# Key products of the sample group: eight of 512 columns over all eight pages instead of sixteen of 256 in two halves

## What is computed

```python
pidx = jnp.minimum(idx, past - 1)
phys = page_table[jnp.arange(Bd)[:, None, None], pidx // ps]
ks = jnp.where(in_past, cache_k[l, phys, off], gather_rows(k_new, nidx))
...
logits = jnp.einsum('bqhd,bqkhd->bqhk', q, ks).astype(jnp.float32) * HEAD_DIM ** -0.5
logits = jnp.where(valid[:, :, None, :], logits, NEG_INF)
p = jax.nn.softmax(logits, axis=-1).astype(vs.dtype)
return jnp.einsum('bqhk,bqkhd->bqhd', p, vs)
```

## Time and profile before

| | |
|---|---|
| median of 3 runs | 1124.06 us (1121.25 to 1125.43) |
| profiled execution, own time | 1125.45 us |
| span of the profiled execution | 1123.7 us |
| TensorE busy | 1038.7 us, 92% |
| VectorE busy | 625.8 us, 56% |
| ScalarE busy | 291.6 us, 26% |
| key products, line 1588 | 1024 instructions, 65.6 us busy |
| value products, line 1652 | 1024 instructions, 69.4 us busy |
| page loads | 512 of 256 KB; 4.4 us (keys) and 4.5 us (values) from issue to landing, median |

### The profile page before, as it was taken

How to read it: one execution, slowest core, us unless ns; L and a number is a source line. 1 busy time by engine, 2 the same in 40 slices (tenths; PEclk the granted TensorE clock), 3 DMA queues, 4 the chain that set the end, 5 groups by cost and what they waited for, 6 DMA issues and landing times.

```text
span 1123.7 us, 18202 instructions
## 1 busy us (share of the span) xinstructions
PE 1038.7 (92%) x6082; PEld 536.1 (48%) x6082; DVE 625.8 (56%) x1999; ACT 291.6 (26%) x614; POOL 171.4 (15%) x292
## 2 busy tenths in 40 slices
PE   6999998899989999989999999979999999998994
PEld 3445444344654455555453644434456445554541
DVE  4237995497785244431550779846868825353233
ACT  3221113311322423421422111142114233242131
POOL 9620100011210000001825010000112000000000
PEclk9999999899999989989999999979999998999998
DMA  8534666446866654455643268653688565445511
GB/s 268 161 115 146 198 230 228 135 161 233 303 226 217 210 172 151 145 187 172 196 127 93 97 194 275 195 169 109 219 278 307 179 210 209 150 151 188 183 61 56
DMA packets 106510, 205.24 MB, mean 183 GB/s; under 512 B 15495, under 2 KB 23894, under 8 KB 106418
## 3 DMA queue, kind: packets, MB, share of 16 engines
q1 hardware_dynamic: 87250, 150.25, 39.5%
q0 software_dynamic: 19168, 53.84, 15.3%
HBM read 194.00 MB, written 10.14 MB: 182 GB/s over the span
## 4 chain that ended last, share of the span: by engine, by line
PE 76%; DVE 11%; SPq 4%; ACT 3%; issue 3%; DMA 2%; DVEq 0%; ACTq 0%
PE bank L1485 34%; PE bank L1760 10%; PE bank L1459 6%; PE bank L1588 5%; PE bank L1652 5%; DVE r L1020 3%; SPq L610 3%; PE bank L1788 2%; PE bank L1718 2%; PE bank L1729 2%; DMA pg<-in_cache_k_dram 2%; PE bank L1814 1%; PE bank L1552 1%; PE bank L1700 1%; DVE sh L1114 1%
## 5 line engine op out<-in xcount | busy, mean ns | idle before, releaser
L1485 PE MATMUL bank<-wr,ht 128*128 128x512 f32 (+1 forms) x1024 | 431.3, 576 | 0.3 <-ACT sh L906 0.3
L1485 PEld LDWEIGHTS bank<-wr,ht 128*128 128x128 f32 x1024 | 192.1, 192 | 210.7 <-issue 205.7
L1020 DVE TENSOR_SCALAR_CACHE_REDUCE r<-r,sel_i 128x1088 bf16<-128x1088 f32 (+3 forms) x248 | 187.4, 793 | 3.6
L694 POOL DMA_DIRECT2D wr<-in_w_in_dram x64 | 45.8, 719 | 431.4 <-PE bank L1485 391.6
L610 POOL DMA_DIRECT2D pg<-in_cache_kidx_dram x128 | 68.8, 540 | 49.2 <-issue 44.1
L1459 PE MATMUL bank<-wr,ht 128*64 128x256 f32 (+1 forms) x640 | 74.7, 390 | 1.1 <-DVE ht L1404 1.1
L1652 PE MATMUL bank<-pg,rs 128*32 128x256 f32 x1024 | 69.4, 415 | 0.2 <-DMA pg<-in_cache_v_dram 0.2
L1588 PE MATMUL bank<-pg,r 128*32 128x256 f32 x1024 | 65.6, 396 | 3.9 <-DMA pg<-in_cache_k_dram 2.4
L694 POOL DMA_DIRECT2D wr<-in_w_out_dram x16 | 11.4, 713 | 339.3 <-PE bank L1485 235.8
L1459 PEld LDWEIGHTS bank<-wr,ht 128*64 128x64 f32 x640 | 45.7, 144 | 28.6 <-issue 9.7
L1760 PE MATMUL bank<-wr,gr 128*128 128x512 f32 x128 | 58.1, 596 | 0.0
(11 more groups left out here) (262 smaller groups left out, 1272.6 us busy)
## 6 DMA issues: line engine op xcount, KB each, us to landing
pg<-in_cache_k_dram SPq DMA_DIRECT2D x256, 256.0 KB, 4.4
pg<-in_cache_v_dram SPq DMA_DIRECT2D x256, 256.0 KB, 4.5
wr<-in_w_in_dram POOLq DMA_DIRECT2D x56, 512.0 KB, 4.7
wr<-in_w_out_dram POOLq DMA_DIRECT2D x16, 512.0 KB, 4.6
r<-in_x_prompt_dram SPq DMA_DIRECT2D x8, 512.0 KB, 6.8
pg<-in_cache_kidx_dram POOLq DMA_DIRECT2D x128, 32.0 KB, 2.1
pg<-in_cache_kidx_dram SPq DMA_DIRECT2D x128, 32.0 KB, 2.2
wr<-in_w_in_dram POOLq DMA_DIRECT2D x8, 256.0 KB, 5.4
```

The costliest lines, as they stand in the source:

```text
L694: pool.dma_start(W[n % 2][:, n4 * 2:n4 * 2 + 2, 0:w], src[:, n4 * 2:n4 * 2 + 2, :])\
L1020: ins = nc.vector.tensor_scalar(junk[i][0:m, 0:part.shape[1]], part, sc, None, ALU.is_ge, ALU.add, accum_out=CNT[0:m, i:i + 1])
L1485: mm = pe.matmul(b[0:m, 0:w], HT[:, k, rt * P:rt * P + m], weights[k], start=(k == 0), stop=(k == KC - 1))
```

## The change

The step waits for all four groups at its start, makes eight products of 512 columns, each over all eight page places of the ring for its sequence (four pieces of 128 columns), and adds 4 to `page_group_used` after the last one. The new view `KEYS` names these places. Nothing else moves: the value steps, the loads and the list are the same.

```diff
+        KEYS = pg[:, :].rearrange("p (u t e c n) -> p u t e c n", u=2, t=2, e=2, c=NC4)
...
                 bk = act_bank(l, "s", p, j)
-                for u in range(2):
-                    two = []
+                for g in range(4):
+                    assert group(l, GROUP[s] + g) == 2 * g
+                for k in range(2):
                     for par in range(2):
-                        s0 = group(l, GROUP[s] + 2 * u + par)
-                        two.append(pg[:, s0 * DA:(s0 + 2) * DA].rearrange("p (e c n) -> p e c n", e=2, c=NC4))
-                    for k in range(2):
-                        for par in range(2):
-                            for e in range(2):
-                                r0, q0 = par * NS + e * HW, (2 * p + par) * NS + e * HW
-                                mm = pe.matmul(bk[r0:r0 + HW, u * 256:(u + 1) * 256], QBX[:, 2 * e + k, q0:q0 + HW],
-                                               two[par][:, :, 2 * e + k, :], start=(k == 0), stop=(k == 1),
-                                               tile_position=(0, r0), skip_group_check=True)
-                            if k == 1:
-                                mm.then_inc(group_used, 1)
+                        for e in range(2):
+                            r0, q0 = par * NS + e * HW, (2 * p + par) * NS + e * HW
+                            mm = pe.matmul(bk[r0:r0 + HW, :], QBX[:, 2 * e + k, q0:q0 + HW], KEYS[:, :, par, :, 2 * e + k, :],
+                                           start=(k == 0), stop=(k == 1), tile_position=(0, r0), skip_group_check=True)
+                mm.then_inc(group_used, 4)
```

## The result

The changed kernel takes **1131.03 us** (median of 7 runs, 1129.80 to 1138.13) against 1124.06 us before (7 runs, 1120.74 to 1127.17). The ratio is 1.0078, with a 95% interval of 1.0054 to 1.0103: it is slower, by 0.8%. Forecast were 1135.4 us and slower. The profiled execution took 1131.03 us, its span is 1129.3 us, 5.6 us more than before.

The account below looks back on a forecast made before the run. TensorE was taken as the bound (76% of the chain). Waits 8.4 - products 0.3 + clock 3.2 = +11.3 us on 1125.45 us gave 1136.8 us; with the runs' median 1.4 us lower, 1135.4 us, range 1127 to 1142.

Parts of the forecast that it names:

- The shape of the products: Key steps: 4 rounds of 512 columns instead of 8 of 256 save 0.01 us a step, 0.3 us in all.
- Rival 3: Key products: fixed cost per instruction decides, saving at most 4.6 us; not slower, perhaps faster (1120.3 us); chance 0.06.
- rival 4: Key products: reading four separate 128-column pieces runs slower; at half the rate 55 us more, 1190 us; chance 0.02.
- The late release: After each key step pages are given back 0.87 us later, so all landings after it move by 0.87 us.
- The waits: Key steps wait for late pages at eight places, four in each layer: +8.4 us in sum.
- the eight steps that were named: Key steps at 107.85, 145.11, 172.33, 392.86, 655.93, 693.18, 720.13 and 939.93, each starting or ending 0.21 to 1.74 us later.
- The step at 107.85: Second key step: last page landing at 108.4 before the change, start moved to 109.45, +1.60 us.
- The cover of the value steps: Value steps after key steps: four longer waits, 3.5 us, hidden by later waits for ACT and VectorE, costed at nothing.
- The clock: TensorE after the two long stands at 145.11 and 693.18: one half-clock stretch each, +3.2 us.
- two possible stretches elsewhere: Half-clock stretches possible after 1.6 to 1.8 us stands at 107.85 and 939.93, set against ones perhaps lost at VectorE waits.
- Rival 1: Key steps stall for pages but bring no extra half-clock time: 1132.2 us; chance 0.24.
- Rival 2: Page landings don't move; only the hoisted wait costs, +4.0 us less 0.3: 1127.8 us, no change; chance 0.18.

Follow-up runs that it names:

- the second trace: The changed kernel run once more without edit, for a second profile: median 1133.72 us, ratio 1.0059 to the kernel before; that trace's span is 1133.4 us.
- The parts: Two kernels, each the kernel before with one edit: release only after the last product, 1126.94 us; wait for all groups at the start only, 1129.79 us.
- the kernel with both parts and 256 columns: The kernel before with the wait at the start and the release at the end, still sixteen products of 256 columns: 1136.35 us, ratio 1.0085.

## Why the prediction was right, and the step of it that wasn't

**The shape of the products: right.** 0.01 us a step forecast, 0.010 us measured (1.864 and 1.854 us), and nothing in the sum of the kernel. The Trainium skill (TensorEngine Tiling (Array Packing), Instruction Overhead) gives about 60 cycles of overhead for each matmul. The runs don't bear that out for products of this size: with 512 instructions fewer and no waits for pages the two kernels are 0.1 us apart, give or take 0.5 us, not an estimated 3.2 or 12.8 us. Rival 3 falls with it, and rival 4 too, as the four-piece read costs nothing.

**The late release: right.** Forecast 0.87 us, measured 0.89 us (2.12 us after the start instead of 1.23), alone and in the changed kernel.

**The waits: right in place, a little small.** 8.4 us forecast, less 0.3 us for the shape; 9.3 us measured at the full clock. Stands for key pages were forecast at some 10 us; they are 10.0 and 12.9 us in two traces. All the eight steps that were named wait for pages in the second trace, seven of them in the first, and no other key step does. This term is the one that was sized too small. The step at 107.85 shows why: forecast 1.6 us later, and in the second trace 2.3 us. Each step's stream was taken from one trace (8.7 us at this step), when the same stream takes 8.3 us in one execution and 9.4 us in another. The parts were forecast at 2.5 us and 4.0 us alone and measured 2.8 us and 4.8 us.

**The cover of the value steps: right.** The timeline that answers to the earlier trace rows:

```profile
308.56 1.92 PE L1586 MATMUL bank<-pg,r 128*32 128x512 f32 x16 [0.15 <-ACT gr L840]
...
321.06 1.07 PE L1648 MATMUL bank<-pg,rs 128*32 128x256 f32 x16 [1.83 <-DMA pg<-in_cache_v_dram]
...
327.88 0.72 PE L1810 MATMUL bank<-cst,r 128*128 128x128 f32 x2 [0.76 <-DVE r L1218]
328.44 7.03 PE L1486 MATMUL bank<-wr,ht 128*128 128x512 f32 x16
335.40 1.92 PE L1586 MATMUL bank<-pg,r 128*32 128x512 f32 x16
```

The value step waits 1.83 us, more than the 1.04 us forecast (0.16 and 0.88), and the wait for VectorE shrinks from 2.45 to 0.76 us, by 1.69 us. The 0.76 us for ACT at the key step before shrinks to 0.15 us. What is lost ahead is given back behind: 1.67 us more at the value step, 1.69 us less at the wait for VectorE. The key step ahead of them starts at 308.56, 4.2 us later than before; the one behind them starts at 335.40, only 2.5 us later. The 1.7 us between these two are the clock's: the tile at 328.44 takes 7.03 us where it took 8.73 us at the half clock.

**The clock: wrong.** This is the step that failed: +3.2 us forecast, -1.4 us measured (half of the difference in half-clock time, 91.2 ± 1.1 us against 93.9 ± 0.7 us in the mean). The rise that was forecast lies well outside; the fall is hardly clear of its error, and the kernel with both parts and 256 columns has 96.4 ± 2.6 us. I took every stand over 2 us to be followed by a stretch at the half clock, as all four were in the trace of before. But that trace has 15 such stretches, some 96 us in all, and those at the four stands are only 20.5 us of it; stands of 1.7 us (at 643.73 and 739.40) had one too. Of the two new stands the first was followed by one, the second was not. Granted clock of the changed kernel, columns as in the earlier trace rows:

```profile
149.04:152.46 3.42, 3.41 (x16) 0.65 (x16) 3.18 (x11) 0.00 (x0) 0.00 (x0) 0.50 0.31 121
...
698.00:705.00 7.00, 4.85 (x24) 1.94 (x24) 6.54 (x19) 1.19 (x2) 0.70 (x1) 1.00 0.68 217
```

The second stretch holds the stand of 2.15 us that ends at 700.17, and the clock stays at 2.4 GHz. The kernel with both parts and 256 columns has the longest stand, 3.10 us, and the clock stays up after it too:

```profile
151.30:158.00 6.70, 6.67 (x43) 3.32 (x44) 6.25 (x18) 0.60 (x1) 0.00 (x0) 1.00 0.57 184
```

In the six traces with the wait or the release moved there are 27 stands of 1.4 us or more for key or value pages. Of the 13 of 2 us or more 6 are followed by a half-clock stretch, of the 14 shorter ones none. The stand of 2.14 us at the prompt's turning (at 491.78 and 1038.46 in the kernel before) has one in every trace, twice. What differs is what TensorE does around it: whole tiles around the page stands, short matmuls and small waits around the other. That this difference is the reason is argued, not shown. The shorter waits for VectorE at 323.64 and in layer 1, which I had set against two possible stretches elsewhere, did come out as a gain: both lost their half-clock stretch. Where the wait stays between 2.39 and 2.82 us in the traces of the other kernels, 7 of 13 have a stretch behind them; in the two traces of the changed kernel, at 0.6 to 1.1 us, none of 4 has. The length matters there, but it doesn't decide alone.

So the forecast of 1135.4 us was 4.4 us high: the waits 1.2 us short (9.3 against 8.1), the clock 4.6 us long (3.2 + 1.4), which leaves 1.0 us to the scatter of executions. The mechanism of the slowdown, late pages at the eight named steps, was right; that the total came out as near as it did is in part luck, since the two errors have opposite signs. Rival 1, the stalls without the clock (1132.2 us), came nearest. Rival 2 fell with the run of the late release, in which landings moved.

## What to carry to other kernels

A wait that is moved ahead and a release that is moved back cost what their sum takes over the slack of each step, not what each costs alone; find it by listing, for all uses of a ring, when the last piece landed and when it was needed. A ring that one step fills wholly has a shortest period: release to first load, the stream, and landing to start; where less work lies between two steps, swapping it about only moves the stand. Merging matmuls of 256 columns into ones of 512 gained nothing here. A stand for a buffer costs its own length, less what a later wait for another engine gives back; a half-clock stretch behind it followed 6 of 13 stands of 2 us or more and isn't to be counted as certain.

## What was new about the hardware

The scatter of this kernel, 1120 to 1133 us in 76 executions, goes mostly with the time at the half clock: a correlation of 0.89 between the two, and at the full clock the mean is known to 0.2 us. I had not expected differences of 1.4 us in 1124 us to be within reach, nor that a stand of 3.1 us leaves the clock up when one of 2.1 us elsewhere brings it down. The length of a stream of eight page loads differs from one execution to the next by 0.5 us and more, from 7.8 to 12.1 us over the places of one trace.
